# A router rebuilt: raw x turned per token tile, the modulation folded around the logits, and two more slots for expert weights

## The reference

```python
hx2 = rms_norm(x, norm2) * (1 + sc2) + sh2          # sc2, sh2: one row each, from the conditioning
g_logits = t @ w_rg + b_rg                          # 4 groups
e_logits = (t @ w_re + b_re)                        # 32 experts, 8 in a group
# top-1 group; top-2 of its 8 experts; weights = softmax(group) * softmax(top 2)
for e in range(N_EXPERTS):
    he = jax.nn.silu(t @ w_gate[e]) * (t @ w_up[e])
    y = y + combine[:, e:e + 1] * (he @ w_down[e])
x = x + g2 * y
```

## Time and profile before

| | |
|---|---|
| median of 3 runs | 1954.29 us (1951.84, 1954.29 and one of 4834.58) |
| the profiled execution's own time | 1952.21 us |
| its span | 1950.4 us |
| granted TensorE clock, mean | 0.979 of 2.4 GHz |
| busy: PE, weight loads, DVE, ACT, POOL | 95%, 73%, 46%, 37%, 5% |
| DMA over the span | 441.85 MB, 227 GB/s |
| the chain that ended last, by engine | PE 76%, DMA 14%, DVE 4%, ACT 3% |

### The profile page before, as it was taken

The page is one execution under the profiler, slowest core; times in us unless marked ns, Lnnn a source line. Parts: engine busy times, 40 slices in busy tenths (PEclk is TensorE's granted clock), DMA queues, the critical chain, the costliest instruction groups (busy, mean ns, idle before and its releaser), DMA issues.

```text
span 1950.4 us, 29881 instructions
## 1 busy us (share of the span) xinstructions
PE 1845.8 (95%) x11572; PEld 1423.1 (73%) x11572; DVE 891.2 (46%) x1313; ACT 727.2 (37%) x1165; POOL 107.2 (5%) x110
## 2 busy tenths in 40 slices
PE   5999699999999969999999999999999998899998
PEld 2876444444344449998899997799989997759998
DVE  4243312222222254545777774545555454635454
ACT  3353122122121133444555553444444443634443
POOL 1010000000000000000221211000000001200000
PEclk8999799999999989999999999999999999999999
DMA  9865299999999966665755442466566665026663
GB/s 371 300 240 200 86 408 422 422 422 422 422 422 422 422 213 184 189 187 152 221 151 137 129 129 65 130 187 179 150 194 182 178 184 206 1 65 194 186 180 108
DMA packets 316421, 441.85 MB, mean 227 GB/s; under 512 B 10821, under 2 KB 269509, under 8 KB 288453
## 3 DMA queue, kind: packets, MB, share of 16 engines
q1 hardware_dynamic: 313528, 431.59, 63.9%
q0 software_dynamic: 2560, 8.40, 1.2%
q10 hardware_dynamic: 272, 1.05, 0.1%
HBM read 439.95 MB, written 1.05 MB: 226 GB/s over the span
## 4 chain that ended last, share of the span: by engine, by line
PE 76%; DMA 14%; DVE 4%; ACT 3%; POOL 1%; issue 1%; SPq 0%; DVEq 0%; POOLq 0%; ACTq 0%
PE PS L255 25%; DMA R<-w_up 13%; PE PS L265 12%; PE PS L349 10%; PE PS L1853 6%; PE PS L1520 4%; PE PS L1914 2%; PE PS L636 1%; PE PS L1042 1%; PE PS L1629 1%; PE PS L1833 1%; PE PS L421 1%; DMA R<-w_ada 1%; PE PS L1177 1%; PE PS L495 1%
## 5 line engine op out<-in xcount | busy, mean ns | idle before, releaser
L255 PE MATMUL PS<-XH,HI 128*128 128x256 f32 x1408 | 400.3, 284 | 3.3 <-DVE XL L129 1.8
L255 PE MATMUL PS<-XL,HI 128*128 128x256 f32 x1408 | 398.5, 283 | 0.0
L255 PE MATMUL PS<-XH,LO 128*128 128x256 f32 x1408 | 398.5, 283 | 0.0
L255 PEld LDWEIGHTS PS<-XH,HI 128*128 128x128 f32 x1408 | 269.7, 192 | 9.0 <-DVE LO L189 2.3
L255 PEld LDWEIGHTS PS<-XL,HI 128*128 128x128 f32 x1408 | 269.8, 192 | 3.8
L255 PEld LDWEIGHTS PS<-XH,LO 128*128 128x128 f32 x1408 | 269.8, 192 | 0.0
L189 DVE TENSOR_TENSOR LO<-RAW,HI 128x2048 fp32r<-128x2048 f32 x84 | 192.6, 2293 | 117.2 <-ACT HI L178 117.2
L198 ACT ACTIVATE HI<-RAW 128x1024 fp32r<-128x1024 f32 x88 | 93.7, 1065 | 293.0 <-PE PS L265 293.0
L222 DVE TENSOR_TENSOR LO<-RAW,HI 128x1024 fp32r<-128x1024 f32 x88 | 107.8, 1225 | 194.5 <-ACT HI L198 194.5
L1853 PE MATMUL PS<-SPLIT,ARENA 128*64 128x512 f32 x512 | 170.0, 594 | 13.1 <-DMA R<-w_up 13.1
L178 ACT ACTIVATE HI<-RAW 128x2048 fp32r<-128x2048 f32 x88 | 167.9, 1908 | 3.0 <-DMA RAW<-ffn_w_in 1.5
(11 more groups left out here) (335 smaller groups left out, 2940.3 us busy)
## 6 DMA issues: line engine op xcount, KB each, us to landing
RAW<-ffn_w_in SPq DMA_DIRECT2D x176, 512.0 KB, 5.1
R<-w_down SPq DMA_DIRECT2D x64, 1024.0 KB, 17.7
RAW<-w_gate SPq DMA_DIRECT2D x48, 1024.0 KB, 20.3
SPLIT<-w_up SPq DMA_DIRECT2D x48, 1024.0 KB, 23.5
RAW<-ffn_w_out SPq DMA_DIRECT2D x88, 512.0 KB, 3.6
RAW<-a_w_in SPq DMA_DIRECT2D x69, 512.0 KB, 5.3
R<-w_ada SPq DMA_DIRECT2D x24, 1024.0 KB, 7.5
SPLIT<-w_gate SPq DMA_DIRECT2D x16, 1024.0 KB, 23.4
```

Source lines behind the costliest of these rows:

```text
L255: m = e.matmul(GU[j][:, T * q:T * q + T], gu(w, j)[:, q, k, :], x[:, k, :], start=(k == 0 and n == 0), stop=(k == KT - 1 and n == 2))
```

## The change

- **The router works on raw x.** The root (a factor of each token) and the modulation (a factor and a term of each channel) are taken around the logits: `WRS` is the router's weights times (1 + sc2) times norm2, `BALL` is the row sh2 @ W + bias spread over the partitions (`router_row`, `router_bias`), and the logits are root * (x @ WRS) + BALL. So TensorE turns x itself, tile by tile (`turn_x`): tile 0 between the third and the fourth group, tile 1 after the fourth. `WRS`, `BALL` and their parts are made by VectorE ahead of its first update of x. The router's weights are loaded with the channels in another order.
- The scaled x of tile 0 (`moe_XN[:, 0]`) is written by VectorE between its updates of x, that of tile 1 by ScalarE; ScalarE copies the turned tile 0 out of PSUM, VectorE tile 1. GpSimd makes the root per tile. The matmuls that spread the second gate come after the second group.
- **Shorter chains.** The masked logits are one addition for both tiles; `KEY` is one operation on `IOTA` values from 1 up; the count and the flag are made after the first one-hots (`counts`); `hot` is one operation a tile and not two.
- **Two more slots** (`MORE`: `XT2` and `SLOT14`) take the first two pieces of the second step, once the router's matmuls and the square of x are done. The later pieces of that step go to the twelve slots as before. `NFR` is loaded after all weights.
- `gate_up` waits for the gathered tokens half by half; TensorE's first two looped steps stand written out.

The diff, cut:

```diff
-        sp.dma_start(M.WR, A["w_router"].rearrange("(p k) n -> p k n", p=128)).then_inc(M.small2, 16)
+        sp.dma_start(M.WR, A["w_router"].rearrange("(k p) n -> p k n", p=128)).then_inc(M.small2, 16)
...
-            a.activation(M.G1B[:, 512 * q:512 * q + 512], FB[0], ACT.Copy).then_inc(s.gb_done, 1)
+            dst = (M.G1B, M.G2B)[q // 2]
+            a.activation(dst[:, 512 * (q % 2):512 * (q % 2) + 512], FB[0 if q < 2 else q - 2], ACT.Copy).then_inc(s.gb_done, 1)
...
+        r = Chain(v, M.moe.rt)
+        v.wait_ge(M.moe.rows_in, 16 * 12)
+        v.wait_ge(s.ch, 17)
+        r.add(v.scalar_tensor_tensor(M.MSC[:, 2], M.MSC[:, 2], 1.0, M.N2, ALU.add, ALU.mult))
+        r.add(v.scalar_tensor_tensor(M.SC2, mc[:, 32:40, 0], 1.0, M.GC[:, GC_N2:GC_N2 + KT], ALU.add, ALU.mult))
+        v.wait_ge(M.small2, 64)
+        r.add(v.tensor_scalar(M.IOTA, M.IOTA, 1.0, None, ALU.add))
+        r.wait()
+        v.wait_ge(s.fo_full, 4)
+        r.add(v.tensor_tensor(M.WRS, M.WR, M.SC2.unsqueeze(2).broadcast_to([128, KT, N_GROUPS + EXPERTS]), ALU.mult))
+        v.wait_ge(M.moe.lg_full, 1)
+        r.add(v.tensor_tensor(M.BROW[0:1], PS[0:1, 7, 0:N_GROUPS + EXPERTS], M.BR[0:1], ALU.add))
+        v.wait_ge(M.moe.lg_full, 2)
+        r.add(v.tensor_copy(M.BALL, PS[:, 7, 64:64 + N_GROUPS + EXPERTS]))
         for n4 in range(4):
+            if n4 == 2:
+                v.wait_ge(s.rs, 4)
+                v.wait_ge(s.xu, 4)
+                v.tensor_scalar(M.moe_XN[:, 0].rearrange("p (k q) -> p k q", k=KT), M.X[:, 0].rearrange("p (q k) -> p k q", k=KT),
+                                M.RS[:, 0:1], None, ALU.mult).then_inc(s.tm, 1)
...
+        def router_row():
+            e.wait_ge(M.small2, 64)
+            mc = M.MC[:].rearrange("p (f w) -> p f w", w=2)
+            for k in range(KT):
+                mm = e.matmul(PS[0:1, 7, 0:NL], mc[:, 24 + k, 0:1], M.WR[:, k, :], start=k == 0, stop=k == KT - 1)
+            mm.then_inc(M.moe.lg_full, 1)
+
+        def router_bias():
+            e.wait_ge(M.moe.rt, 5)
+            e.matmul(PS[:, 7, 64:64 + NL], M.ONES[0:1, :], M.BROW[0:1], start=True, stop=True).then_inc(M.moe.lg_full, 1)
+
+        def turn_x(t, banks):
+            for k in range(KT):
+                mm = e.transpose(PS[:, banks[k // 4], 128 * (k % 4):128 * (k % 4) + 128], M.X[:, t, 128 * k:128 * k + 128], M.ID[:])
+                if k % 4 == 3:
+                    mm.then_inc(s.turned, 1)
+
+        def router(t):
+            for k in range(KT):
+                mm = e.matmul(PS[:, 2 + t, 0:NL], M.XT2[:, k, 128 * t:128 * t + 128], M.WRS[:, k, :],
+                              start=k == 0, stop=k == KT - 1)
+            mm.then_inc(M.moe.lg_full, 1)
 
...
+                router_row()
+            if n4 == 1:
+                e.wait_ge(s.gb_done, 2)
+                for q in range(2):
+                    row = 32 * (2 + q)
+                    e.matmul(FB[q], M.ONES[row:row + 1, :], M.MR[row:row + 1, 2, :], start=True, stop=True).then_inc(s.gb_full, 1)
+                router_bias()
+            if n4 == 2:
+                e.wait_ge(s.xu, 4)
+                e.wait_ge(M.moe.rt, 6)
+                turn_x(0, (6, 7))
+        e.wait_ge(s.xh, 2 * KT + 2)
+        e.wait_ge(s.xu, 6)
+        router(0)
+        e.wait_ge(s.xu, 8)
+        turn_x(1, (0, 1))
+        e.wait_ge(s.tm, 2 * KT + 3)
+        router(1)
...
+    MORE = [M.XT2.rearrange("p k t -> p (k t)"), M.SLOT14]
...
+        def step_loads(i, odd, r, done=0):
+
+            for m in range(done, LOADS):
                 sp.wait_ge(s.used, i * (2 * LOADS) + (LOADS * (PAIR_STEPS * r + odd - 1) + m + 1))
                 load(i * 2 + odd, m)
...
+                M.router_read(sp)
+                for m in range(len(MORE)):
+                    load(1, m, MORE[m], M.mix.w_first[m])
+                step_loads(0, 1, 0, done=len(MORE))
             for r in range(first // PAIR_STEPS, end // PAIR_STEPS):
                 with sp.Fori(0 if r else 1, PAIR_STEPS // 2) as i:
                     step_loads(i, 0, r)
                     step_loads(i, 1, r)
+            if first == 0:
+                sp.dma_start(M.NFR, A["norm_final"]).then_inc(M.mix.cx_in, 16)
...
-                for x in range(2):
-                    v.tensor_scalar(M.OH[:, par, t, CAP * x:CAP * x + CAP], M.IOTA, KEY[:, t, bass.ds(it * 2 + x, 1)], None,
-                                    ALU.is_equal).then_inc(s.oh, 1)
+                v.tensor_tensor(M.OH[:, par, t].rearrange("p (x c) -> p x c", x=2), M.IOTA.unsqueeze(1).broadcast_to([128, 2, CAP]),
+                                KEY[:, t, bass.ds(it * 2, 2)].unsqueeze(2).broadcast_to([128, 2, CAP]),
+                                ALU.is_equal).then_inc(s.oh, 1)
...
+            start = isinstance(i, int) and i == 0
+            if m < len(MORE) and start and odd:
+                e.wait_ge(M.mix.w_first[m], 32)
+                return MORE[m]
+            earlier = 32 if m < len(MORE) and not start else 0
+            e.wait_ge(s.w_in[m // 2], i * (2 * 32) + (32 * odd + 32 - earlier))
             return SLOTS[m]
 
         def gate_up(i, odd):
             it = i * 2 + odd
-            e.wait_ge(s.xg_done, it * 8 + 8)
             at_least(e, s.h_done, it)
             if not isinstance(it, int) or it > 1:
                 e.wait_ge(s.acc, it * 4 - 4)
             for m in range(0, 8, 2):
                 w = [w_loaded(i, odd, m + x) for x in range(2)]
+                if m < 4:
+                    e.wait_ge(s.xg_done, it * 8 + (4 + 2 * m))
...
+            if first == 0:
+                two_steps(0)
+            with e.Fori(first // 2 or 1, end // 2 - 1) as i:
+                two_steps(i)
...
+            if t == 0:
+                for b in range(2):
+                    a.wait_ge(M.mix.turned, KT + b + 1)
+                    a.activation(M.XT2[:, 4 * b:4 * b + 4, 0:128], PS[:, 6 + b, :].rearrange("p (k n) -> p k n", k=4),
+                                 ACT.Copy).then_inc(M.mix.xh, 1)
+        a.wait_ge(M.mix.rs, 6)
+        a.activation(XN[:, 1].rearrange("p (k q) -> p k q", k=KT), M.X[:, 1].rearrange("p (q k) -> p k q", k=KT),
+                     ACT.Copy, scale=M.RS[:, 1:2]).then_inc(M.mix.xh, 1)
...
+        for t in range(NT):
+            r = M.RS[:, t:t + 1]
+            p.wait_ge(M.mix.sq, 4 + t + 1)
+            p.tensor_scalar(r, M.SS[:, t:t + 1], 1 / D, EPS, ALU.mult, ALU.add).then_inc(M.mix.rs, 1)
+            p.wait_ge(M.mix.rs, 2 * t + 3)
+            p.tensor_tensor(r, r, M.HF[:, 0:1], ALU.pow).then_inc(M.mix.rs, 1)
...
-        v.wait_ge(M.mix.xu, 8)
-        v.wait_ge(s.rows_in, 16 * 12)
-        n.add(v.scalar_tensor_tensor(M.MSC[:, 2], M.MSC[:, 2], 1.0, M.N2, ALU.add, ALU.mult))
-        v.wait_ge(M.mix.rs, 4)
-        for t in range(NT):
-            n.add(v.tensor_scalar(XN[:, t].rearrange("p (k q) -> p k q", k=KT), M.X[:, t].rearrange("p (q k) -> p k q", k=KT),
-                                  M.RS[:, t:t + 1], None, ALU.mult))
+        n = Chain(v, s.rt, 6)
+        for b in range(2):
+            v.wait_ge(M.mix.turned, KT + 2 + b + 1)
+            v.tensor_copy(M.XT2[:, 4 * b:4 * b + 4, 128:256], PS[:, b, :].rearrange("p (k n) -> p k n", k=4)).then_inc(M.mix.tm, 1)
         n.wait()
-        for k in range(KT):
-            v.wait_ge(M.mix.turned, KT + k // 2 + 1)
-            v.tensor_scalar(M.XT2[:, k], TRB[k // 2][:, T * (k % 2):T * (k % 2) + T], M.MSC[:, 2, k:k + 1],
-                            M.SH2[:, k:k + 1], ALU.mult, ALU.add).then_inc(M.mix.tm, 1)
-        v.wait_ge(s.lg_full, 1)
-        n.add(v.tensor_copy(M.LG, PS[:, 0, 0:NT * NL]))
+        v.wait_ge(M.mix.rs, 6)
+        for t in range(NT):
+            v.wait_ge(s.lg_full, t + 3)
+            n.add(v.scalar_tensor_tensor(lg[:, t], PS[:, 2 + t, 0:NL], M.RS[:, t:t + 1], M.BALL, ALU.mult, ALU.add))
...
-        for t in range(NT):
-            group = lambda ap: ap[:, t].unsqueeze(2).broadcast_to([128, N_GROUPS, EPG])
-            expert = lambda ap: ap[:, t].rearrange("p (g e) -> p g e", e=EPG)
-            step(v.tensor_tensor(expert(EM), expert(el), group(OHG), ALU.mult))
-            step(v.tensor_tensor(expert(EM), expert(EM), group(T4), ALU.add))
+        by_group = lambda ap: ap.rearrange("p t (g e) -> p t g e", e=EPG)
+        step(v.tensor_tensor(by_group(EM), by_group(el), T4.unsqueeze(3).broadcast_to([128, NT, N_GROUPS, EPG]), ALU.add))
...
-        step(v.tensor_tensor(OH1, OH1, OH2, ALU.add))
+        n.add(v.tensor_tensor(CW[:, :, 0:EXPERTS], OH1, OH2, ALU.add))
         v.wait_ge(s.rk_full, 1)
-        step(v.tensor_reduce(M.CNT, PS[0:1, 1, 64:96], axis=AX.X, op=ALU.max))
-        v.tensor_scalar(M.FLAG[0:1, 0:1], M.CNT, float(CAP), None, ALU.is_gt).then_inc(s.counted, 1)
-
         v.wait_ge(s.sel, 1)
-        step(v.tensor_scalar(T32, by_tile(PS[:, 1, 0:64]), 1.0, None, ALU.add))
-        step(v.tensor_tensor(T32, T32, EM, ALU.mult))
-        n.add(v.tensor_scalar(KEY[:, :, 0:EXPERTS], T32, -1.0, None, ALU.add))
```

(60 more changed lines are left out.)

27 lines of the change are left out of this document (13 added, 14 removed).

## The result

The changed kernel takes 1938.09 us (median of 4 runs, 1936.95 to 1942.99) against 1954.20 before (median of 4 runs; 1954.11 without the one of 4834.58). The medians differ by 16.1 us; the ratio over the runs is 0.9931, with a 95% interval of 0.9919 to 0.9943: 11 to 16 us less, 13.5 by its middle, well under 2% of the time. The forecast was 1942: 10.7 us less than the 1952.2 of the profiled execution, with half the distance to the median added. The profiled execution took 1936.95 us.

What follows compares the result with a forecast made beforehand. The unbroken weight stream was taken to end the expert stage: first expert product 8.35 us earlier plus 2.3 in the stream, 10.7 off 1952.2, gives 1941.5, or 1942 with half the distance to the median; range 1934 to 1950.

Steps and rivals of the forecast that it cites:

- thin work ahead of Y: Shift-term row, second-gate spread, bias row and first transposes among the projection groups: 4.4 us later end of the fourth group.
- Y to reduction: From the first x update behind the fourth group to the first router reduction: 17.9 us before, 5.1 net gained at the reduction.
- mask, key, one-hot: Shorter VectorE chains while experts are picked: 0.65 us from the mask, 0.9 from the key, 0.2 from the one-hot.
- first products ahead of the second half: First expert products no longer wait for the second half of ScalarE's gather copies: 1.5 us earlier.
- stream behind G: Weight stream after the first expert product: 4.97 preloaded plus 1.24 norm_final, less 3.44 later start and 0.5 break, 2.3 us gained.
- Rival (d): The expert stage's end is set by something the router doesn't move, so time stays at 1952 us; chance 0.07.
- +1.65: Extra us for tile 1's router products behind the last dense group, taken at 3.63 us because the clock falls.
- 6.3 at full clock: Us from the end of the fourth group to the first router reduction if the clock doesn't fall.
- rival (a): Router products and gather stay fast and the stream goes well: 12.7 to 14 us gained, 1939 us; chance 0.15.
- (b): A new wait replaces the removed one, from late x updates or costlier thin work between groups: 5 us lost, 1946.5; chance 0.15.
- (c): Thin work between projection groups halves the clock, +6.9 us per dense group: 1948.4 for one, 1962 for three; chance 0.08.
- Edits costed at nothing: Router weights read in 1024 small pieces, TensorE's first two steps written out, GpSimd's root per tile: all taken as free.

Runs made afterwards that it cites:

- e0: The changed kernel run once more with no edit; median 1936.38 us.
- e3: The changed kernel, but gate_up waits for all eight gathered pieces of x before its first product, in every step; median 1942.72 us.
- e5: The changed kernel plus unused filler products (128x256), six behind the last router products and one behind the rank products; median 1936.17 us.
- e7: The changed kernel plus sixteen unused router-like products (128x36) behind the bias row and again behind the first turn of x; 1947.54 us.
- e8: The changed kernel with the first turn of x moved behind the fourth group, and both sets of router products behind the turns; median 1937.97 us.
- e9: The changed kernel with the first turn behind the fourth group and filler products, eight behind the last router products, two behind the rank products; median 1935.31 us.
- e6: The changed kernel plus filler: six products behind the last router products, one behind the rank products, two between second turn and last router products; median 1938.69 us.
- e4: The changed kernel without the two extra slots, with norm_final back in the weight stream and gate_up waiting for all gathered x; median 1943.05 us.
- e10: The changed kernel with the two extra slots given to the second step's pieces 8 and 9 (down), not 0 and 1 (gate); median 1935.60 us.
- e1: The changed kernel without the two extra slots, the second step's pieces 0 and 1 going to ordinary slots again; median 1940.27 us.

## Why the prediction was right

The span fell by 15.3 us in the two profiles. By the steps of the prediction:

| step | predicted | measured (before and after) |
|---|---|---|
| start of the first group | 0 | -0.85, chance (176.1 to 178.9) |
| thin work ahead of Y | +4.4 | +2.74 |
| Y to reduction | 17.9 to 8.4, -9.5 | 17.87 to 7.47, -10.4 |
| mask, key, one-hot | -1.75 | -1.82 |
| first products ahead of the second half | -1.5 | -0.38, of which the gather +1.28 |
| stream behind G | -2.3 | -2.82 |
| dense layers | 0 | -1.8, chance (1251 to 1257) |
| sum | -10.7 | -15.3 |

Without the two rows of chance it is 12.7, 2.0 more than forecast.

**What bounds.** The end of the expert stage is the end of the stream: every change of G went through to F one for one (F - G 454.5 to 454.9 in after, e0, e3, e5, e7, e8, e9, whose G lies between 225.4 and 240.0; 455.5 in e6, whose first wait for w_up already ended at G + 206.8 where the others have 205.5 to 206.1; why stays open). Rival (d) falls.

**The term that was mis-sized** is the first: I took the row for the shift term at 1.8 us, by the rows of 128 columns, where products that load one column took 0.61; and the second gate with the bias row at 1.57 where they ran overlapped in 1.06. Thus Y moved by 2.74 and not 4.4. The turn was 0.87. The four groups themselves took 28.07 in sum (7.06, 7.06, 7.07, 6.88) where they had taken 27.87 with three in a row.

**Behind Y** the chain went as worked out: router products of tile 0 beside the x update, turn, copies, products, one fused op. The clock fell where I had put it, at the last products (3.63 for sixteen instructions), and the turn ahead of it was still fast. In seven further profiles of the same code the same products took 1.98 to 3.19, so the full +1.65 was the slowest case seen, and the first profile happened to have it. Without the fall R - Y is 5.8 (e4, e10: 1.98 for the products), so the "6.3 at full clock" was half a microsecond too careful. Half of rival (a), the fast router products, did occur, in two of eight profiles; its fast gather never did without filler (5.34 to 6.46).

**The short chains** were right to 0.1. **The split wait** is worth 1.7 (e3) against 1.5 predicted; in the profile after, the gather at half clock hid most of it, which I had left out of the sum as a matter of where the clock changes. **The stream**: the extra slots 1.6 (predicted 4.97 - 3.44 - 0.5 = 1.0), norm_final 1.5 (1.24); the start at G + 7.1 and the break at G + 23 both stand in the profile. But the close agreement of 2.8 with 2.3 is in part luck. At the last wait but one for w_up the kernel before stands at G + 416.3 and the changed one at G + 414.4 (643.62 - 229.18): the start, the bytes and the break brought 1.9. The other 0.9 came in the last step, for which the prediction had no term; 0.7 of it is the last wait for w_up, which took 26.18 us in the kernel before, where the eight before it took 25.5:

```profile
630.72 25.50 DMA R<-w_up
...
660.54 26.18 DMA R<-w_up
```

Why the last step was longer there, and in e1, stays open.

**Rivals.** (b), DVE late for the third group, didn't occur: it was ready 0.8 us ahead. (c) didn't occur, and e7 showed that it would with sixteen more thin products behind the bias row. The rule of the Trainium skill on transposes (TensorE: Matmul & The Clock Gate, Part 4: PE-mode transpose) would have had the full clock not engage for the turn; here the turn stood between groups at full clock, the windows of the turn and of the fourth group behind it show 1.00 (200 to 202), and with Y - M at 31.76 or 31.77 in all nine executions the fourth group never lost time by it. **Edits costed at nothing**: the router weights in small pieces and the steps written out show no cost (M lies on both sides of before's 176.97, F - G shrank by no less than worked out), but neither was tried by itself. For the router weights, SP's issue of the four bias loads behind them took 5.04 us and not 1.80, and the load behind those was issued at 65.55 as before (65.58): 3.2 us, near the "two or three" for which the prediction gave no row, and covered by the queue.

The range held because the clock's two levels were in it; the gain beyond the forecast is 2.8 us of 13.5 by the ratio: the first term (1.7), the stretch behind Y (0.9) and the stream (0.5) less the slow gather (1.1) make 2.0 of it, and the rest is within the interval.

## What to carry to other kernels

When a stage ends with a stream of transfers, ask only what moves its start, its bytes and its breaks, and follow the release of buffers piece by piece: two slots of 5 us brought 1.6, because the first wait moved to a later release, and giving the same slots to the pieces that are released last brought 1.1 more. Work moved ahead of a stage pays only where the engine doesn't wait behind it: the early turn moved 0.9 us out of a wait. Where single executions vary by 6 us, compare terms of the chain between fixed points and not whole times.

## What the runs showed of the hardware

- Eight fp32 products (sixteen instructions) with one column of weights and 36 moving columns took 0.61 us; eight with 128 columns of weights took 1.87 to 1.98 at full clock and 3.63 at half.
- The granted clock fell at different points of the same thin stretch from run to run: R - Y 5.8 to 7.5, the gather 5.3 to 6.5 us, identical code. In e7 it fell during 32 thin instructions (128x36) between dense groups, which took 4.91 us, and the next dense group took 9.33 in place of 7.1; the same 32 ahead of the next group took 3.66 and the clock stayed at 1.00.
- Products whose results nobody reads, put in an idle of five microseconds, brought the clock back to 1.00 ahead of the gather (3.81 us) in one profile (e5); in another (e6), where they ran faster and so ended sooner, the clock fell again and the gather took 6.09.
